# First norm's result stored by contraction chunk and left unscaled, read with unit steps by the router's transposes and the gather

## The reference

```python
x = layer_norm(alpha * x + mix, ln1_g, ln1_b)
ffn = hierarchical_moe(x, ...)      # group top-1 of 4, expert top-2 of 8; 32 gated-MLP experts of 1024 x 256
x = layer_norm(alpha * x + ffn, ln2_g, ln2_b)
```

## Time and profile before

| | |
|---|---|
| median of 3 runs | 471.78 us (471.65 to 472.29) |
| span of the profiled execution | 472.3 us; no other time of its own is given, and the longest run is 472.29 us |
| TensorE busy | 418.4 us (89%) |
| VectorE / ScalarE / GpSimd busy | 158.4 / 120.2 / 15.0 us |
| weight loads busy | 307.1 us (65%) |
| DMA moved | 134.63 MB, mean 285 GB/s |
| mean granted TensorE clock | 0.942 |

### The profile page before, as it was taken

The page is one execution under the profiler, slowest core; times in us unless marked ns, Lnnn a source line. Parts: engine busy times, 40 slices in busy tenths (PEclk is TensorE's granted clock), DMA queues, the critical chain, the costliest instruction groups (busy, mean ns, idle before and its releaser), DMA issues.

```text
span 472.3 us, 7099 instructions
## 1 busy us (share of the span) xinstructions
PE 418.4 (89%) x2741; PEld 307.1 (65%) x2742; DVE 158.4 (34%) x307; ACT 120.2 (25%) x198; POOL 15.0 (3%) x37
## 2 busy tenths in 40 slices
PE   7899899999999998979999796897894896899998
PEld 6899898988999997855473362273442452455647
DVE  3554577864555654682110010010010010011116
ACT  4454546444444442202110010010010010011010
POOL 2000000000000001130000000000000000000004
PEclk9999999999999999997999898699997897799899
DMA  8787979664777679990999999999999999999902
GB/s 277 199 278 240 315 228 304 225 219 132 246 226 247 216 230 315 299 349 17 302 348 380 353 349 381 350 348 382 348 348 382 349 349 382 298 366 348 379 7 89
DMA packets 124065, 134.63 MB, mean 285 GB/s; under 512 B 8080, under 2 KB 106384, under 8 KB 124048
## 3 DMA queue, kind: packets, MB, share of 16 engines
q1 hardware_dynamic: 123472, 132.30, 85.9%
q0 software_dynamic: 576, 2.10, 1.1%
HBM read 133.33 MB, written 1.05 MB: 285 GB/s over the span
## 4 chain that ended last, share of the span: by engine, by line
PE 45%; SPq 35%; DVE 9%; issue 4%; DMA 4%; ACT 3%; POOL 0%; ACTq 0%; DVEq 0%
SPq L319 24%; PE bank L935 20%; SPq L324 8%; PE bank L1127 6%; PE bank L1151 5%; PE bank L1052 4%; DMA dn<-in_w_down 3%; PE bank L1029 2%; PE bank L1183 2%; PE bank L1176 2%; SPq L346 2%; DVE wl L644 2%; DMA raw<-in_w_in 1%; ACT wh L501 1%; SPq L301 1%
## 5 line engine op out<-in xcount | busy, mean ns | idle before, releaser
L644 DVE TENSOR_TENSOR wl<-raw,wh 128x1024 fp32r<-128x1024 f32 x56 | 68.3, 1224 | 68.1 <-ACT wh L501 67.9
L935 PE MATMUL bank<-xh,wh 128*128 128x256 f32 x288 | 82.9, 288 | 3.5 <-DVE wl L644 1.9
L935 PE MATMUL bank<-xl,wh 128*128 128x256 f32 x288 | 81.5, 283 | 0.0
L935 PE MATMUL bank<-xh,wl 128*128 128x256 f32 x288 | 81.4, 283 | 0.0
L501 ACT ACTIVATE wh<-raw 128x1024 fp32r<-128x1024 f32 x56 | 58.7, 1056 | 62.9 <-PE bank L935 40.5
L1127 PEld LDWEIGHTS bank<-pick,x 128*128 128x128 f32 x288 | 70.0, 335 | 4.2 <-issue 1.9
L1127 PE MATMUL bank<-pick,x 128*128 128x128 f32 x288 | 69.2, 401 | 1.3 <-DVE pick L824 1.3
L1176 PE MATMUL bank<-dn,hT 128*32 128x512 f32 x256 | 42.2, 801 | 29.4 <-DMA dn<-in_w_down 29.4
L1151 PE MATMUL bank<-gu,xg 128*32 128x512 f32 x512 | 61.6, 637 | 7.4 <-issue 7.4
L935 PEld LDWEIGHTS bank<-xh,wh 128*128 128x128 f32 x288 | 55.2, 192 | 6.2 <-issue 3.7
L935 PEld LDWEIGHTS bank<-xl,wh 128*128 128x128 f32 x288 | 55.2, 192 | 0.2 <-issue 0.2
(11 more groups left out here) (182 smaller groups left out, 425.8 us busy)
## 6 DMA issues: line engine op xcount, KB each, us to landing
dn<-in_w_down SPq DMA_DIRECT2D x64, 512.0 KB, 8.9
gu<-in_w_gate SPq DMA_DIRECT2D x32, 768.0 KB, 9.6
gu<-in_w_up SPq DMA_DIRECT2D x32, 768.0 KB, 10.0
raw<-in_w_in SPq DMA_DIRECT2D x40, 512.0 KB, 4.6
gu<-in_w_gate SPq DMA_DIRECT2D x32, 256.0 KB, 6.8
gu<-in_w_up SPq DMA_DIRECT2D x32, 256.0 KB, 7.6
raw<-in_w_o SPq DMA_DIRECT2D x8, 512.0 KB, 4.6
raw<-in_w_out_conv SPq DMA_DIRECT2D x4, 512.0 KB, 3.5
```

What stands on the lines that cost most here:

```text
L644: dve.tensor_tensor(wl[:, s, :].rearrange("p (k c) -> p k c", k=KC), raw[:, pair % NRAW, :].rearrange("p (k c) -> p k c", k=KC) [:, :, n % ...
L935: mm = pe.matmul(dst, w[:, k, :], v[:, i, :], start=(i == 0 and w is h and v is high_in), stop=(i == len(ks) - 1 and w is l))
```

## The change

x1 keeps its size but its free dimension is grouped by chunk: `x1n` is a view of it, channel p*8 + k at place k*128 + p. ScalarE and VectorE write the first norm's result through that view, in output runs of one element with a step of 128. Transposes and gather then take `x1[:, t, k*P:(k+1)*P]`. x1 is no longer scaled in place; the scaled and shifted rows that the second seeding needs go to a new tile `xa`, which lies over pickw and what follows it. VectorE does tile 0, GpSimd both halves of tile 1, waiting for the norm and no longer for the transposes. The gather's result is scaled and shifted as it leaves PSUM, by the columns gcol and bcol: four ScalarE and four VectorE instructions of 128 columns take the place of one each. VectorE waits for the seeding (`added`) before it first writes pickw. The last merge runs by token tile, and the router's matmuls and transposes stand in another order.

```diff
+        xa_scope = ExitStack()
+        xa = sb("xa", [P, TT, DM], where=xa_scope)
+        xa_scope.close()
...
+        x1n = x1[:, :, :].rearrange("q t (k p) -> q t p k", k=KC)
...
                 if n == 0:
-                    cols = slice(HALF, DM)
                     pool.wait_ge(ln_in, 32)
-                    pool.wait_ge(x1T_ps, 4)
-                    link(pool.tensor_tensor(x1[:, 1, cols], x1[:, 1, cols], lng[:, cols], ALU.mult))
-                    pool.tensor_tensor(x1[:, 1, cols], x1[:, 1, cols], lnb[:, cols],
-                                       ALU.add).then_inc(x1_done, 1)
+                    for h in range(2):
+                        cols, rows = slice(h * HALF, (h + 1) * HALF), slice(h * P // 2, (h + 1) * P // 2)
+                        pool.wait_ge(norm_done[1], h + 1)
+                        link(pool.tensor_tensor(xa[:, 1, cols].rearrange("q (p k) -> q p k", k=KC),
+                                                x1n[:, 1, rows, :],
+                                                lng[:, cols].rearrange("q (p k) -> q p k", k=KC), ALU.mult))
+                        pool.tensor_tensor(xa[:, 1, cols], xa[:, 1, cols], lnb[:, cols],
+                                           ALU.add).then_inc(x1_done, 1)
...
             for h in range(2):
-                act.activation(x1[:, 0, h * HALF:(h + 1) * HALF], bank[h][:, :], ACT.Identity,
+                act.activation(x1n[:, 0, h * P // 2:(h + 1) * P // 2, :],
+                               bank[h][:, :].rearrange("q (p k) -> q p k", k=KC), ACT.Identity,
                                scale=rstd[:, 0:1], bias=shift[:, 0:1]).then_inc(norm_done[0], 1)
...
                 act.wait_ge(xg_ps, 2 * n - 1)
-                act.activation(xg[:, 0:KC // 2, :], bank[4][:, :].rearrange("p (k s) -> p k s", s=P),
-                               ACT.Copy).then_inc(xg_a, 1)
+                for k in range(KC // 2):
+                    ins = act.activation(xg[:, k, :], bank[4][:, k * P:(k + 1) * P], ACT.Identity,
+                                         scale=gcol[:, k:k + 1], bias=bcol[:, k:k + 1])
+                ins.then_inc(xg_a, 1)
...
-                dve.tensor_scalar(x1[:, 1, h * HALF:(h + 1) * HALF], bank[2 + h][:, :], moments[:, 1, 0:1],
+                dve.tensor_scalar(x1n[:, 1, h * P // 2:(h + 1) * P // 2, :],
+                                  bank[2 + h][:, :].rearrange("q (p k) -> q p k", k=KC), moments[:, 1, 0:1],
                                   rstd[:, 1:2], ALU.subtract, ALU.mult).then_inc(norm_done[1], 1)
...
-            for t, cols in ((0, slice(0, DM)), (1, slice(0, HALF))):
-                dve.wait_ge(x1T_ps, 2 * t + 2)
-                link(dve.tensor_tensor(x1[:, t, cols], x1[:, t, cols], lng[:, cols], ALU.mult))
-                dve.tensor_tensor(x1[:, t, cols], x1[:, t, cols], lnb[:, cols],
-                                  ALU.add).then_inc(x1_done, 1)
+            dve.wait_ge(norm_done[0], 2)
+            link(dve.tensor_tensor(xa[:, 0, :].rearrange("q (p k) -> q p k", k=KC), x1n[:, 0, :, :],
+                                   lng[:, :].rearrange("q (p k) -> q p k", k=KC), ALU.mult))
+            dve.tensor_tensor(xa[:, 0, :], xa[:, 0, :], lnb[:, :], ALU.add).then_inc(x1_done, 1)
...
-                dve.tensor_copy(xg[:, KC // 2:KC, :],
-                                bank[5][:, :].rearrange("p (k s) -> p k s", s=P)).then_inc(xg_v, 1)
+                for k in range(KC // 2, KC):
+                    ins = dve.tensor_scalar(xg[:, k, :], bank[5][:, k % 4 * P:(k % 4 + 1) * P],
+                                            gcol[:, k:k + 1], bcol[:, k:k + 1], ALU.mult, ALU.add)
+                ins.then_inc(xg_v, 1)
...
+            dve.wait_ge(added, 2 * TT)
             weigh_slots(1, 0)
...
+                rows = xa if signal else x1
                 for t in range(TT):
                     for h in range(2):
-                        mm = pe.matmul(bank[2 * t + h][:, :], alpha_i[:, :], x1[:, t, h * HALF:(h + 1) * HALF],
+                        mm = pe.matmul(bank[2 * t + h][:, :], alpha_i[:, :], rows[:, t, h * HALF:(h + 1) * HALF],
...
-            for m in range(2):
-                merge(JP - 1, m, 2, False)
+            for t in range(TT):
+                merge(JP - 1, 0, 2, t)
+                merge(JP - 1, 1, 2, t).then_inc(acc_done, 1)
...
                     mm = pe.transpose(bank[4 + 2 * t + k // 4][:, (k % 4) * P:(k % 4 + 1) * P],
-                                      x1[:, t, k::KC], ident[:, :])
+                                      x1[:, t, k * P:(k + 1) * P], ident[:, :])
...
             transpose_tile(0)
+            logits(0, 0)
+            logits(0, 1)
             pe.wait_ge(bias_read, 1)
-            logits(0, 0)
             transpose_tile(1)
-            logits(0, 1)
             logits(1, 0)
...
-                        mm = pe.matmul(bank[4 + k // 4][:, (k % 4) * P:(k % 4 + 1) * P], x1[:, t, k::KC],
+                        mm = pe.matmul(bank[4 + k // 4][:, (k % 4) * P:(k % 4 + 1) * P],
+                                       x1[:, t, k * P:(k + 1) * P],
```

More of the change, by code:

```diff
@@ L1071, in _ @@
                 for m in range(2):
-                    merge(j, m, 6)
+                    merge(j, m, 6, 0)
+                    merge(j, m, 6, 1).then_inc(unit_done, 1)
             for m in range(2):
                 branches(JP - 1, m)
-            for m in range(2):
-                merge(JP - 1, m, 2, False)
+            for t in range(TT):
+                merge(JP - 1, 0, 2, t)
+                merge(JP - 1, 1, 2, t).then_inc(acc_done, 1)
             pe.wait_ge(y_done, KC)
```

24 lines of the change are left out of this document (11 added, 13 removed).

## The result

| | before | after |
|---|---|---|
| median (range, executions) | 472.03 us (471.65 to 473.89, 4) | 466.31 us (465.14 to 467.46, 4) |
| ratio | | 0.9881 (95% interval 0.9847 to 0.9915) |
| span of the profiled execution (its own time) | 472.3 us | 464.1 us (465.88) |
| TensorE / weight loads busy | 418.4 / 307.1 us | 379.9 / 270.6 us |
| VectorE / ScalarE / GpSimd busy | 158.4 / 120.2 / 15.0 us | 164.4 / 128.0 / 20.2 us |

Faster, by 5.7 us (1.2%), where 13.6 were forecast. The 0.2% that the prediction took for the measurement was too small: 39 more executions of the kernel before, on three chips, lie between 469.3 and 475.3 us. The profiled spans differ by 8.2 us.

The account below looks back on a forecast made before the run. TensorE's path was taken to bound the kernel until round 0 ends, then the weight stream until near the end. Stream start 5.6 us earlier plus 8.0 at the end made 13.6: 471.78 - 13.6 = 458.2 us, range 455.4 to 464.2.

Parts of the forecast that it names:

- What bounds the kernel: Three stages: TensorE and VectorE to about 210 us, TensorE's path through round 0, then the weight stream until near the end.
- The gather: With unit-step weight loads each gather takes 3.72 us in place of 7.67, or of 7.88 in the first.
- Clock of gate and up: Gate and up products of rounds 0 and 7 run at clock 1.00, saving 1.70 us each.
- Norm to gather: From the first norm to the first gather: start unchanged at 210.3 us, bounds 1.1 earlier and 2.5 later.
- rival 2: Seedings late: GpSimd ends near 208 us, the first gather starts 2.5 us later, total 460.7 us; chance 0.18.
- rival 1: TensorE's clock stays low: up to 1.65 us lost in the gather, 1.70 in round 0, total 462.1 us; chance 0.20.
- Leaving PSUM: VectorE's four pieces behind each gather cost 0.24 us more than one copy, bounds 0 and 0.7; ScalarE's are covered.
- The sum: Weight stream starts 5.6 us earlier, the end from quad 6's down weights saves 8.0: 13.6 us, giving 458.2.
- The norm pieces: First norm's strided writes on ScalarE and VectorE: about 1.3 us per 512 columns, where 0.77 was needed.
- GpSimd's strided reads: Two strided reads in GpSimd's four instructions on xa add 1.3 us to 5.7; GpSimd ends at 205.3 us.

Follow-up runs that it names:

- e1_natural: The changed kernel with its regrouping alone undone (x1 in natural order, transposes and gather again with a step of 8 elements): 476.23 us, ratio 1.0069.
- e5_again: The changed kernel, unaltered, run once more beside the kernel before: 464.14 us, ratio 0.9855.
- e4_fill: The changed kernel with 12 more filler matmuls on TensorE between the last logits and the wait for xa: 462.16 us, ratio 0.9781.
- e2_noxa: The changed kernel without GpSimd's and VectorE's instructions on xa, seeding from unscaled x1, so its result is not the reference's: 462.52 us, ratio 0.9798.
- e6_biasmm: The changed kernel with the addition of ln1_b to xa moved to four float32 TensorE matmuls, no fillers: 462.86 us, ratio 0.9822.
- e10_merge: The changed kernel with 12 fillers and the last merge in its old order (both token tiles of m = 0, then m = 1): 469.0 us, ratio 0.9907.

## Why the prediction was wrong, by its steps

**What bounds the kernel: right.** The three stages held in all fourteen profiles; rounds 1 to 5 gave nothing back, and "to end" is the same within 1.8 us for every unit-step kernel.

**The gather: right.** 192 ns a load, 3.73 and 3.81 us a group, where 3.72 was forecast. The strided gather's pace does not depend on the clock, as argued: 7.88 us at 0.78 in before and 7.88 at 1.00 in `e1_natural`, which shows the step as the cause. No unit-step gather ran at the low clock.

**Clock of gate and up: right in its number.** 7.07 us in rounds 0 and 7, and in 94 of 96 unit-step rounds nothing was lost beyond the waits. That the 1.70 us of round 0 were owed to the slow gather isn't shown, since `e1_natural` didn't lose them there behind a gather as slow.

**Norm to gather: the step that failed.** It said "I take the first gather's start as unchanged at 210.3". Behind the mixer it moved from 23.93 to 26.11, 2.2 us later (26.92 in `e5_again`). The working up to it was good: GpSimd was put at 205.3, which is 18.9 us behind the mixer, and the seedings started at 19.34. What it then did was to issue eight seedings at 0.43 us and to place the ranking at about 208.8, where the old routing chain had put it. Three things were left out:
- The clock. TensorE had nothing to do for 2.9 us behind the logits, where it had waited 1.08 before. The seedings ran at 0.68 and took 5.40 us. `e4_fill` prices this at 1.7 us.
- The routing chain shares the time with GpSimd. I gave VectorE nothing to gain against 203.98; the logits were added 1.1 us earlier (16.50 against 17.58), and all of it and 0.4 more went again into the two small steps held up by GpSimd. `e2_noxa` and `e6_biasmm` have `chosen` 1.6 us earlier. In after itself this cost nothing, since the ranking waited 1.9 us more for the seedings; in `e4_fill` both are out of the way when the ranking starts, `chosen` only 0.15 us before it.
- The seedings stand ahead of the ranking. Even at clock 1.00, 19.3 and 8 x 0.43 is 22.8, where the ranking of `e4_fill` is (22.86), 0.5 later than before.

This is rival 2 (seedings late, gather 2.5 us later) by its effect and place. Its cause was half rival 1, which had put the low clock in the gather and in round 0, where it did not appear; it was in the one group that neither looked at. Nor did GpSimd end near 208, as rival 2 had it: that is 21.6 us behind the mixer, and it ended at 19.3. Rival 2 had 0.18; taken as the likeliest, it gave 460.7.

**Leaving PSUM: mis-sized.** 0.24 us was forecast, 0.68 measured, close to the upper bound (0.7), which stood for four pieces without overlap. The pace was taken from `pick` writes; VectorE's pieces with scale and shift out of PSUM last 403 ns and four take 1.36 us. ScalarE's four take 1.50 us and end inside the gather, as said.

**The sum.** Up to the stream 5.6 us were forecast and 2.9 came: 2.2 by the late gather, 0.5 by the exit and the gather's 0.09 us. From the down weights of quad 6 to the end 8.0 were forecast and 7.2 came: the second half of the last down products started 43.0 us behind that issue (405.86 to 448.85), where 42.2 were forecast. That was a misreading of the rows of before. The prediction ended its stream at 448.7, from the share of 0.69, but the next microsecond still moved data:

```profile
449.00:450.00 1.00, 1.00 (x12) 0.27 (x8) 0.00 (x0) 0.00 (x0) 0.00 (x0) 1.00 0.12 45
```

There the last down weights were issued at 438.4 and took up to 11.7 us to land, so until 450.1 or 43.3 us behind quad 6's issue; in after 437.1 and 11.7 give 448.8, or 42.9. The stream's end had not moved against its issue, only been read a microsecond too early. The hole behind the issue isn't the reason, since before has it too (mean share 0.75 in its first 4 us, 0.70 in after). Another 0.2 lies in the rounds between. Together 3.7, and 13.6 - 3.7 = 9.9, the gain behind the mixer that the profiles show.

Between 9.9 and the 5.7 of the medians lies no step of the change. 1.7 us are the longer mixer of after's profiled execution, 0.7 the distances of the two profiled executions from their medians (472.29 from 472.03, 465.88 from 466.31). The last 1.75 are the difference between time and span, which 465.88 has against its 464.1 and 472.29 has not against its 472.3. So the steps alone would have left the forecast at 458.2 + 3.7 = 461.9, inside its range; the other 4.4 us of the miss are executions and this frame. Of the 3.7 that belong to the steps, the late gather is the largest part, 2.2.

**The norm pieces** took 1.12 us (ScalarE) and 1.08 (VectorE) where 1.3 was taken (512 columns at the 1.9 ns named there are 0.97), and the wide multiplication 2.50. The Trainium skill's Vector Engine (DVE) Microarchitecture Reference, Measured stream behaviour on trn2, gives 1.7 to 2.5 ns a column for such steps; the trace agrees, with 1.08 us / 512 = 2.1 ns and 2.50 / 1024 = 2.4, the latter beside a busy GpSimd (1.75 in the natural layout). **GpSimd's strided reads** took 1.52 us where the natural layout has 1.27:

```profile
198.31 1.27 POOL L485 TENSOR_TENSOR xa<-x,lng 128x512 f32<-128x512 f32 x1 [0.99 <-DVE x L777]
```

That is 20% more; the second multiplication took 2.49 against 2.25 us. VectorE worked beside all four, so the share of the step alone isn't shown. The Trainium skill's GPSIMD Engine Reference, Performance pitfalls for Q7 kernels, gives 50% for reads stepping over 8 bytes; here one of two operands steps, and the measurement decides.

## What to carry to other kernels

A float32 operand that TensorE loads as weights many times should be stored once with unit steps: the writer's stride was paid once, at 0.3 to 0.4 us for each of four pieces, and the loads of every gather ran at twice the pace. When work moves to a slower engine, look at who waits for it in a queue, what stands behind that wait, and how long TensorE then has nothing to do; one line of fillers bought back 1.7 of the 3.4 us that the work on `xa` cost. And take the scatter of the profiled execution out of the comparison with a common mark, such as the end of an untouched stage, before reading small differences, and see that both times are taken in the same way.

## What the runs showed of the hardware that I had not expected

- The granted clock can fall at short idle stretches, at a high price. 2.92 us without work ahead of the seedings cost 1.7 us in them (5.40 against 3.70 us, and 6.25 in `e5_again`), and filling that stretch took the price away (`e4_fill`). 1.55 us in `e1_natural` were followed by the same 5.40 us. 1.46 us ahead of the transposes of `e10_merge` were followed by 13.7 us at 0.50, which cost 5.2 us in three groups alone.
- The length of the stretch doesn't decide by itself: 1.08 us ahead of before's seedings cost nothing, nor 1.25 ahead of the first gather of after, nor 1.60 us in each round with unit-step gathers, while the same 1.60 us behind strided ones went with slow products in 5 of 8 rounds of `e1_natural`. What does decide stays open.
- VectorE and GpSimd hold each other up even where the operands are small: VectorE's step on 128 x 8 took 0.98 us beside GpSimd and 0.17 alone, GpSimd's contiguous addition 2.76 us beside VectorE's multiplication and addition on `xa` and 1.26 beside its small steps.
- The transposes' loads, 198 ns at a step of 32 bytes, fell to 146 at unit step, so they had paid something too; but nowhere near the gather's 335. Why the same step costs the two so differently stays open.
